# Low parts of moving operands placed 64, 128 or 192 bytes further on

## The chip, the cores and the metric

One core of a Trainium2 chip runs the whole program. The metric is the device time of one launch in microseconds; the median of three runs of the kernel before is 2188.57 us (2188.35 to 2189.26).

## The reference

Two transformer-like blocks run one after the other on 256 tokens of width 2048, all in float32:

```
first block:  h = rmsnorm(x); proj = h @ w_in          # 16 k-tiles of 128
              y_pool, y_conv, y_attn = three mixers of parts of proj
              mixed = sum_n sigmoid(h @ w_gate[n] + b) * (y_n @ w_branch[n]);  x += rmsnorm(mixed @ w_out)
              h = rmsnorm(x); m = relu(h @ w_up)^2 @ w_down;  x += rmsnorm(m)
second block: h = modulated rmsnorm(x); q, k, v, gates from h @ w_in_2; attention; Fourier mix
              out = rmsnorm(x + gate * ((g_a*y_a + g_b*y_b) @ w_out_2))
```

## The kernel before

Every large product is made in three passes of a reduced float32 format (float32r): each operand is kept as a high part and a low part (what is missing from the high part to the exact value), and high times high, high times low and low times high are added up in PSUM. A weight chunk is 256 rows by 512 columns; it comes by DMA into `raw`, ScalarE writes its high part (line 964) and VectorE its low part (line 1318). The order of the chunks is a fixed list of jobs, and small pieces of other work (transposes, softmax, attention scores) are put between chunks at places that the program works out beforehand.

A job has one of two modes. In mode T the activations are the stationary operand and 512 weight columns move through the array (lines 910 to 912). In mode W the weights are the stationary operand, 128 columns at a time, and the 256 tokens of the activations move ("pass the weights", lines 917 to 919):

```
917  pe.matmul(o, wh, xh[:, ka, :], ...)
918  pe.matmul(o, wh, xl[:, ka, :], ...)
919  pe.matmul(o, wl, xh[:, ka, :], ...)
```

`xh` and `xl` are looked up by the job's operand name in `hi_of` and `lo_of` (lines 404 to 407). Each of the 128 partitions of SBUF has its own addresses, and all that follows is about addresses in bytes within a partition, taken modulo 256. `line(64)` moves the allocation to the next address that is 64 past a multiple of 256. From that, the places are:

- the activations' high and low parts (`op0h`, `op0l`, `op1h`, `op1l`, and `yah`, `hch`, `mgh` with their low parts): 64;
- weights in mode T, high and low: 64;
- weights in mode W: high parts 128, low parts 0;
- `tmp` and the small tensors behind it: 64, the attention tensors `qt`, `ktx` and others: 64.

The low parts are written by VectorE: of x0 on line 1386, of x1 and x2 on line 1404, of the pool and conv operands on lines 1490 and 1713. x0, x1 and x2 are the operands of the first block's projections, of its MLP and of the second block; they use the same buffers one after the other. x1 is used in 16 jobs of mode W, x2 in 12 of mode W and in 6 of mode T, pool and conv in 4 each of mode W with half as many k-tiles.

Of the kernel before, what the change touches and what calls it, by code (L numbers as in the profile page):

```python
# [12 lines left out]
F32 = mybir.dt.float32  # L13
F32R = mybir.dt.float32r
# [119 lines left out]
def program(nc, a, out, scratch_e, scratch_x):  # L134
    ctx = ExitStack()
    with ctx:
# [159 lines left out]
        top = [(nc.sbuf_base + 63) // 64 * 64]  # L296

        def at(name, shape, off, dt=F32):
            return nc.alloc_sbuf_tensor_at(name, shape, dt, offset=off)

        def sb(name, shape, dt=F32):
            size = 4 * int(np.prod(shape[1:]))
            t = at(name, shape, top[0], dt)
            top[0] += (size + 31) // 32 * 32
            return t

        raw = [sb(f"raw{i}", [128, KC, 512]) for i in range(NRAW)]
        def line(shift):

            top[0] += (shift - top[0]) % 256  # L310
            return top[0]
# [11 lines left out]
        whi, wlo = split_buffers("whi", 64), split_buffers("wlo", 192)  # L323
        op0_at = line(64)
        op0h, op0l = sb("op0h", [128, 16, 256], F32R), sb("op0l", [128, 16, 256], F32R)
        op1_at = line(64)
        op1h, op1l = sb("op1h", [128, 16, 256], F32R), sb("op1l", [128, 16, 256], F32R)
        tmp_at = top[0]
        tmp = [sb(f"tmp{i}", [128, 512]) for i in range(6)]
        ident = sb("ident", [128, 128])  # L330
# [15 lines left out]
        def bg(name, shape, kb, dt=F32):  # L346
            return at(name, shape, big + int(kb * 1024), dt)
# [18 lines left out]
        x0 = bg("x0", [128, 2, 2048], 52)  # L366
# [12 lines left out]
        hch, hcl = bg("hch", [128, 16, 256], 40, F32R), bg("hcl", [128, 16, 256], 56, F32R)  # L379
# [23 lines left out]
        fgb = at("fgb", [128, 2048], op1_at)  # L403
        hi_of = {"x0": op0h, "x1": op0h, "x2": op0h, "pool": op1h, "conv": op1h, "mix": op1h, "hid0": op1h, "hid1": op1h, "hid2": op1h,
                 "hid3": op1h, "att": op1h, "four": op1h, "ya": yah, "ctx": hch, "mg": mgh}
        lo_of = {"x0": op0l, "x1": op0l, "x2": op0l, "pool": op1l, "conv": op1l, "mix": op1l, "hid0": op1l, "hid1": op1l, "hid2": op1l,
                 "hid3": op1l, "att": op1l, "four": op1l, "ya": yal, "ctx": hcl, "mg": mgl}

        columns = {}
# [15 lines left out]
        def half(ps):  # L425
            return ps[:, :].rearrange("p (k t) -> p k t", k=2)
# [3 lines left out]
        def sem(name):  # L430
            return ctx.enter_context(nc.semaphore("s_" + name))
# [20 lines left out]
        s_winr, s_pwm, s_psc, s_phi, s_plo = sem("pool_window"), sem("pool_weight"), sem("pool_scaled"), sem("pool_high"), sem("pool_operand")  # L452
        s_cy, s_chi, s_clo = sem("conv_taps"), sem("conv_high"), sem("conv_operand")
# [853 lines left out]
        def _(v):  # L1307
# [75 lines left out]
            def low_x0(u, j):  # L1383
                k = 2 * u + j
                v.wait_ge(s_x0hi, k + 1)
                i = v.scalar_tensor_tensor(op0l[:, k, :], bank[4 + k % 4][:, 0:256], vat[:, k:k + 1], op0h[:, k, :].bitcast(F32), ALU.mult, ALU.subtract)
                if j:
                    i.then_inc(s_oper, 1)
                elif u == 0:
                    i.then_inc(s_oper0, 1)  # L1390

            def turn_x(u):
                if u < 8:
                    low_x0(u, 0)
                    low_x0(u, 1)
                    return
                s, k = u // 8, 2 * (u % 8)
                h, l, x = (op0h, hch)[s == 1][:, k:k + 2, :], (op0l, hcl)[s == 1][:, k:k + 2, :], half(tmp[2 + u % 2])
                if u == 8:
                    v.wait_ge(s_pe, of["b23"].end)  # L1400
                v.wait_ge(s_turned, u - 7)
                v.tensor_copy(h, x).then_inc(own.sem, own.up())
                v.wait_ge(own.sem, own.n)
                v.tensor_tensor(l, x, h.bitcast(F32), ALU.subtract).then_inc(s_oper, 1)
# [82 lines left out]

            def pool_low(g):
                v.wait_ge(s_phi, g + 1)
                v.tensor_tensor(op1l[:, 2 * g:2 * g + 2, :], half(tmp[5]), op1h[:, 2 * g:2 * g + 2, :].bitcast(F32), ALU.subtract).then_inc(s_plo, 1)  # L1490

            def conv_taps(b, c):
                ct, job = 4 * b + c, of[f"cc{b}"]
# [168 lines left out]
            def fourier_d(g):  # L1662
# [3 lines left out]
                else:  # L1666
# [9 lines left out]
                v.tensor_tensor(op1l[:, 12 + g, :], tmp[5][:, 0:256], op1h[:, 12 + g, :].bitcast(F32), ALU.subtract).then_inc(s_four, 1)  # L1676

            parts = {"vectors_b": vectors_b, "bias_row": bias_row, "index_sum": index_sum, "top_rounds": top_rounds, "pool_window": pool_window, "pool_low": pool_low, "conv_taps": conv_taps,
                     "softmax1_max": softmax1_max, "softmax1_scale": softmax1_scale, "values1": values1, "fold_map": fold_map, "ada_quarters": ada_quarters,
                     "ada_columns": ada_columns, "ctx_var": ctx_var, "ctx_norm": ctx_norm, "ctx_turn": ctx_turn, "row_var": row_var, "row_norm": row_norm, "turn_x": turn_x, "x1_add": x1_add, "mlp_add": mlp_add,  # L1680
                     "turn_qk": turn_qk, "split_kc": split_kc, "rotate": rotate, "softmax2_max": softmax2_max, "softmax2_less": softmax2_less, "softmax2_sum": softmax2_sum,
                     "softmax2_share": softmax2_share, "values2": values2, "values2_low": values2_low, "fourier_d": fourier_d}
# [20 lines left out]
            def ep_cb(job, b0, b1):  # L1703
                blk = job.arg
                if blk:
                    v.wait_ge(s_chi, 2)
                v.wait_ge(s_cy, 4 * blk + 4)
                for i, b in ((0, b0), (1, b1)):
                    v.tensor_tensor(half(tmp[2 + i]), half(b), cu[:, 2 * i:2 * i + 2, :], ALU.mult).then_inc(s_pair[job.pair], 1)
                for i in range(2):  # L1710
                    k = 8 + 4 * blk + 2 * i
                    v.wait_ge(s_chi, 2 * blk + i + 1)
                    v.tensor_tensor(op1l[:, k:k + 2, :], half(tmp[2 + i]), op1h[:, k:k + 2, :].bitcast(F32), ALU.subtract).then_inc(s_clo, 1)

            def ep_br(job, b0, b1):
                n, c = job.arg
# [131 lines left out]
            def ep_o2_last(job, b0, b1):  # L1848
# [14 lines left out]
                def columns(i):  # L1863
# [27 lines left out]
                v.tensor_scalar(X2[:, 1, 768:1536], X2[:, 1, 768:1536], rs, None, ALU.mult).then_inc(s_fin, 1)  # L1891

            eps = {"copy": ep_copy, "vw": ep_vw, "cc": ep_cc, "cb": ep_cb, "br": ep_br, "wo": ep_wo, "up": ep_up, "dn": ep_dn, "qk": ep_qk,
                   "silu": ep_silu, "pb": ep_pb, "pa": ep_pa, "o2": ep_o2}

# [26 lines left out]
            low_x0(0, 1)  # L1922
            low(1)
            turn_x(1)
            low(2)
            turn_x(2)
            x0_norm(0, 1024, 2048)
            x0_norm(1, 1024, 2048)
# [36 lines left out]
```

## Time and profile before

| | |
|---|---|
| median of three runs | 2188.57 us |
| the profiled execution | 2189.04 us |
| its span, first to last instruction | 2187.2 us |
| granted TensorE clock, mean | 0.999 of full speed |
| PE busy | 2177.7 us (100%) |
| VectorE / ScalarE busy | 1548.0 (71%) / 1063.0 us (49%) |
| DMA | 474.97 MB, mean 217 GB/s |

The table is read from the top: the span is some 2 us below the profiled execution's time, and one engine is busy through all of it. Matmuls are pipelined, so that the time of one matmul in the profile is longer than the distance from its start to the start of the next.

### The profile page before, as it was taken

How to read it: one execution, taken by the hardware profiler on the slowest of the kernel's cores; microseconds unless marked ns; L12 is line 12 of the kernel's file. 1: busy time of each engine (PE TensorE's matmuls, PEld its weight loads, DVE VectorE, ACT ScalarE, POOL GpSimd, SP SyncE). 2: the span in 40 equal slices, each digit the busy share in tenths (PEclk: the TensorE clock that was granted, in tenths of full speed). 3: DMA queues.
4: the chain of work that ended last, by engine and by line, in shares of the span. 5: the costliest groups of instructions: out<-in, count | busy, mean ns of one | idle time of the engine just before them, and what ended most of it. 6: DMA issues, size and time to landing. Idle time of an engine off the chain costs nothing.

```text
span 2187.2 us, 37567 instructions
## 1 busy us (share of the span) xinstructions
PE 2177.7 (100%) x15900; PEld 2046.9 (94%) x15900; DVE 1548.0 (71%) x1895; ACT 1063.0 (49%) x1398; POOL 120.0 (5%) x111
## 2 busy tenths in 40 slices
PE   9999999999999999999999999999999999999998
PEld 9999999999999889989988988998889999999987
DVE  7899588888889577544554555555768787777776
ACT  5444445544444566444543443444555555444443
POOL 1000000000000400000000000000101111110001
PEclk9999999999999999999999999999999999999999
DMA  8876676687787956656656656656755545688784
GB/s 275 245 241 200 201 251 220 228 280 258 256 277 265 244 188 184 193 192 194 196 195 193 194 193 196 200 192 203 246 174 164 164 144 170 224 272 282 256 279 155
DMA packets 248480, 474.97 MB, mean 217 GB/s; under 512 B 21974, under 2 KB 26448, under 8 KB 247544
## 3 DMA queue, kind: packets, MB, share of 16 engines
q1 hardware_dynamic: 243032, 454.40, 65.5%
q0 software_dynamic: 5280, 18.17, 2.9%
q8 instruction: 125, 2.05, 0.4%
q14 instruction: 43, 0.35, 0.0%
HBM read 468.30 MB, written 5.78 MB: 217 GB/s over the span
## 4 chain that ended last, share of the span: by engine, by line
PE 97%; DMA 1%; DVE 1%; ACT 0%; issue 0%; SPq 0%; DVEq 0%; POOLq 0%; POOL 0%; ACTq 0%
PE ps L917 21%; PE ps L918 21%; PE ps L919 21%; PE ps L910 10%; PE ps L911 10%; PE ps L912 10%; PE ps L835 1%; DMA raw<-in_w_out 1%; PE ps L758 0%; PE ps L708 0%; DMA raw<-in_w_in 0%; PE ps L745 0%; PE ps L824 0%; PE ps L823 0%; PE ps L825 0%
## 5 line engine op out<-in xcount | busy, mean ns | idle before, releaser
L917 PE MATMUL ps<-op0h,whiW 128*128 128x256 f32 x3376 | 937.3, 278 | 0.1
L919 PE MATMUL ps<-op0h,wloW 128*128 128x256 f32 x3376 | 932.8, 276 | 0.0
L918 PE MATMUL ps<-op0l,whiW 128*128 128x256 f32 x3376 | 932.7, 276 | 0.0
L1318 DVE TENSOR_TENSOR wloW<-raw,whiW 128x1024 fp32r<-128x1024 f32 (+1 forms) x503 | 618.3, 1241 | 313.5 <-ACT whiW L964 311.1
L964 ACT ACTIVATE whiW<-raw 128x1024 fp32r<-128x1024 f32 (+1 forms) x504 | 529.3, 1058 | 586.0 <-PE ps L919 471.2
L917 PEld LDWEIGHTS ps<-op0h,whiW 128*128 128x128 f32 x3376 | 633.8, 188 | 2.5 <-issue 1.3
L918 PEld LDWEIGHTS ps<-op0l,whiW 128*128 128x128 f32 x3376 | 633.9, 188 | 0.6
L919 PEld LDWEIGHTS ps<-op0h,wloW 128*128 128x128 f32 x3376 | 633.8, 188 | 0.0
L1318 DVE TENSOR_TENSOR wloT<-raw,whiT 128x1024 fp32r<-128x1024 f32 (+1 forms) x264 | 319.1, 1217 | 237.7 <-ACT whiT L964 236.5
L964 ACT ACTIVATE whiT<-raw 128x1024 fp32r<-128x1024 f32 (+1 forms) x264 | 274.0, 1046 | 286.2 <-PE ps L912 228.9
L910 PE MATMUL ps<-whiT,op1h 128*128 128x512 f32 x640 | 249.3, 390 | 0.3 <-DVE wloT L1318 0.3
L911 PE MATMUL ps<-wloT,op1h 128*128 128x512 f32 x640 | 249.1, 389 | 0.0
L912 PE MATMUL ps<-whiT,op1l 128*128 128x512 f32 x640 | 249.1, 389 | 0.0
L1345 DVE SCALAR_TENSOR_TENSOR tmp<-raw,csil,tmp 128x512 f32<-128x512 f32 x300 | 209.3, 746 | 1.1
L910 PEld LDWEIGHTS ps<-whiT,op1h 128*128 128x128 f32 x640 | 120.1, 188 | 25.7 <-issue 1.0
L912 PEld LDWEIGHTS ps<-whiT,op1l 128*128 128x128 f32 x640 | 120.1, 188 | 25.0
L911 PEld LDWEIGHTS ps<-wloT,op1h 128*128 128x128 f32 x640 | 120.1, 188 | 24.7
L917 PE MATMUL ps<-op1h,whiW 128*128 128x256 f32 x512 | 141.9, 277 | 0.0
L918 PE MATMUL ps<-op1l,whiW 128*128 128x256 f32 x512 | 141.4, 276 | 0.0
L919 PE MATMUL ps<-op1h,wloW 128*128 128x256 f32 x512 | 141.4, 276 | 0.0
L918 PEld LDWEIGHTS ps<-op1l,whiW 128*128 128x128 f32 x512 | 96.1, 188 | 0.1
L917 PEld LDWEIGHTS ps<-op1h,whiW 128*128 128x128 f32 x512 | 96.1, 188 | 0.1
(314 smaller groups left out, 2106.8 us busy)
## 6 DMA issues: line engine op xcount, KB each, us to landing
raw<-in_w_in SPq DMA_DIRECT2D x256, 512.0 KB, 4.3
raw<-in_w_up SPq DMA_DIRECT2D x128, 512.0 KB, 3.8
raw<-in_w_down SPq DMA_DIRECT2D x128, 512.0 KB, 4.1
raw<-in_w_ada SPq DMA_DIRECT2D x96, 512.0 KB, 4.6
raw<-in_w_gate SPq DMA_DIRECT2D x96, 512.0 KB, 5.1
raw<-in_w_out SPq DMA_DIRECT2D x64, 512.0 KB, 5.3
raw<-in_w_branch SPq DMA_DIRECT2D x48, 512.0 KB, 5.1
raw<-in_w_proj_a SPq DMA_DIRECT2D x24, 512.0 KB, 5.0
```

The costliest lines, as they stand in the source:

```text
L835: mm = pe.matmul(bank[4][:, 256 * e:256 * e + 256], vv[:, st % 2, 128 * kv:128 * kv + 128], keyed[e][:, st, :], start=st == 0, stop=st == 3)
L910: pe.matmul(o, th, h[:, kk, c0:c1], start=first, stop=False, skip_group_check=True)
L911: pe.matmul(o, th, l[:, kk, c0:c1], start=False, stop=False, skip_group_check=True)
L912: mm = pe.matmul(o, tl, h[:, kk, c0:c1], start=False, stop=last, skip_group_check=True)
L917: pe.matmul(o, wh, xh[:, ka, :], start=first and m % 2 == 0, stop=False, skip_group_check=True)
L918: pe.matmul(o, wh, xl[:, ka, :], start=False, stop=False, skip_group_check=True)
L919: mm = pe.matmul(o, wl, xh[:, ka, :], start=False, stop=last, skip_group_check=True)
L964: act.activation(whi[job.mode][q % NSPL][:, :, 0:job.n], raw[i][:, :, 0:job.n], ACT.Copy).then_inc(s_hi, 1)
L1318: v.tensor_tensor(wlo[job.mode][q % NSPL][:, :, 0:job.n], x, h.bitcast(F32), ALU.subtract).then_inc(s_lo, 1)
L1345: op = v.scalar_tensor_tensor(o, w, c, o, ALU.mult, ALU.add)
```

## The change

Three new names lie over the old low buffers, further on by 128, 192 and 64 bytes, and the allocation is moved up by 192 and by 64 bytes so that they have room. The writers on lines 1404, 1490 and 1713 (numbers of before) write to them, and the table `lo_of` gives them to the matmuls. Nothing is added to or taken from any engine's instructions.

```diff
         op0h, op0l = sb("op0h", [128, 16, 256], F32R), sb("op0l", [128, 16, 256], F32R)
+        x1l, x2l = at("x1l", [128, 16, 256], op0_at + 16384 + 128, F32R), at("x2l", [128, 16, 256], op0_at + 16384 + 192, F32R)
+        top[0] += 192
         op1_at = line(64)
         op1h, op1l = sb("op1h", [128, 16, 256], F32R), sb("op1l", [128, 16, 256], F32R)
+        poolcl = at("poolcl", [128, 16, 256], op1_at + 16384 + 64, F32R)
+        top[0] += 64
         tmp_at = top[0]
...
-        lo_of = {"x0": op0l, "x1": op0l, "x2": op0l, "pool": op1l, "conv": op1l, "mix": op1l, ...
+        lo_of = {"x0": op0l, "x1": x1l, "x2": x2l, "pool": poolcl, "conv": poolcl, "mix": op1l, ...
...
-                h, l, x = (op0h, hch)[s == 1][:, k:k + 2, :], (op0l, hcl)[s == 1][:, k:k + 2, :], half(tmp[2 + u % 2])
+                h, l, x = (op0h, hch)[s == 1][:, k:k + 2, :], (op0l, hcl, x1l, x2l)[s][:, k:k + 2, :], half(tmp[2 + u % 2])
...
-                v.tensor_tensor(op1l[:, 2 * g:2 * g + 2, :], half(tmp[5]), ...
+                v.tensor_tensor(poolcl[:, 2 * g:2 * g + 2, :], half(tmp[5]), ...
...
-                    v.tensor_tensor(op1l[:, k:k + 2, :], half(tmp[2 + i]), ...
+                    v.tensor_tensor(poolcl[:, k:k + 2, :], half(tmp[2 + i]), ...
```

After the change the low parts of x1 lie at 192 modulo 256, of x2 at 0, of pool and conv at 128. The first allocation after them, `op1_at`, is again at 64 (256 bytes higher), but `tmp` and the small tensors behind it move from 64 to 128. The large region behind those begins with `line(64)` as before. The mix, MLP-hidden, attention and Fourier operands keep `op1l`.

## Rows read from the trace of the kernel before

**Rows 1.** The page: busy time of the engines, clock in 40 slices.
```profile
PE 2177.7 (100%) x15900; PEld 2046.9 (94%) x15900; DVE 1548.0 (71%) x1895; ACT 1063.0 (49%) x1398; POOL 120.0 (5%) x111
...
PEclk9999999999999999999999999999999999999999
```

**Rows 2.** All that PE waited for, by releaser: total us, times, longest.
```profile
PE ps L931 <- DVE tmp L1910: 1.2, 1, 1.2
PE ps L910 <- DVE wloT L1318: 0.3, 1, 0.3
PE ps L937 <- DMA vst<-in_b_gate: 0.3, 1, 0.3
```

**Rows 3.** Groups of PE instructions by shape: count, busy us, mean ns, idle before.
```profile
L918 PE MATMUL ps<-op0l,whiW 128*128 128x256 f32 x3376 | 932.7, 276 | 0.0
...
L918 PE MATMUL ps<-op1l,whiW 128*128 128x256 f32 x512 | 141.4, 276 | 0.0
...
L912 PE MATMUL ps<-whiT,op0l 128*128 128x512 f32 x192 | 74.9, 390 | 0.0
...
L835 PE MATMUL ps<-keyed,vc 128*128 128x256 f32 x48 | 12.3, 379 | 0.0
...
L912 PE MATMUL ps<-whiT,mgl 128*128 128x256 f32 x32 | 9.0, 282 | 0.0
...
L825 PE MATMUL ps<-qt,op1l 128*128 128x256 f32 x24 | 6.8, 283 | 0.0
```

**Rows 4.** PE by stretch (window, length, busy us, matmuls in it).
```profile
1020.00:1100.00 80.00, 80.00 (x708) 1.00 0.64 197
1965.00:2000.00 35.00, 35.00 (x311) 1.00 0.89 312
...
1110.00:1180.00 70.00, 70.00 (x311) 1.00 0.61 199
...
2174.00:2179.00 5.00, 5.00 (x44) 1.00 0.00 0
```

**Rows 5.** PE in order of time around attention scores (start us, us, instruction).
```profile
1646.26 0.28 PE L917 MATMUL ps<-op0h,whiW 128*128 128x256 f32 x1
...
1646.60 0.28 PE L823 MATMUL ps<-qt,ktx 128*128 128x256 f32 x1
...
1649.36 0.28 PE L825 MATMUL ps<-qt,ktcl 128*128 128x256 f32 x1
1649.47 0.28 PE L917 MATMUL ps<-op0h,whiW 128*128 128x256 f32 x1
...
1649.83 0.28 PE L917 MATMUL ps<-op0h,whiW 128*128 128x256 f32 x1
...
1650.51 0.28 PE L917 MATMUL ps<-op0h,whiW 128*128 128x256 f32 x1
```

**Rows 6.** PE in order of time in a mode-T job of x2.
```profile
1714.80 0.39 PE L910 MATMUL ps<-whiT,op0h 128*128 128x512 f32 x1
...
1716.43 0.39 PE L911 MATMUL ps<-wloT,op0h 128*128 128x512 f32 x1
```

**Rows 7.** The chain that ended last, two merged pieces (start us, us).
```profile
831.33 1.75 PE ps L708 x16
...
1668.72 3.45 PE ps L835 x16
```

**Rows 8.** VectorE: writing low parts, activations' and weights'.
```profile
L1404 DVE TENSOR_TENSOR op0l<-tmp,op0h 128x512 fp32r<-128x512 f32 x16 | 11.1, 693 | 0.5
...
L1318 DVE TENSOR_TENSOR wloW<-raw,whiW 128x1024 fp32r<-128x1024 f32 (+1 forms) x503 | 618.3, 1241 | 313.5 <-ACT whiW L964 311.1
```

More of the change, by code:

```diff
@@ L405, in program @@
                  "hid3": op1h, "att": op1h, "four": op1h, "ya": yah, "ctx": hch, "mg": mgh}
-        lo_of = {"x0": op0l, "x1": op0l, "x2": op0l, "pool": op1l, "conv": op1l, "mix": op1l, "hid0": op1l, "hid1": op1l, "hid2": op1l,
+        lo_of = {"x0": op0l, "x1": x1l, "x2": x2l, "pool": poolcl, "conv": poolcl, "mix": op1l, "hid0": op1l, "hid1": op1l, "hid2": op1l,
                  "hid3": op1l, "att": op1l, "four": op1l, "ya": yal, "ctx": hcl, "mg": mgl}
@@ L1489, in pool_low @@
                 v.wait_ge(s_phi, g + 1)
-                v.tensor_tensor(op1l[:, 2 * g:2 * g + 2, :], half(tmp[5]), op1h[:, 2 * g:2 * g + 2, :].bitcast(F32), ALU.subtract).then_inc(s_plo, 1)
+                v.tensor_tensor(poolcl[:, 2 * g:2 * g + 2, :], half(tmp[5]), op1h[:, 2 * g:2 * g + 2, :].bitcast(F32), ALU.subtract).then_inc(s_plo, 1)
             def conv_taps(b, c):
@@ L1712, in ep_cb @@
                     v.wait_ge(s_chi, 2 * blk + i + 1)
-                    v.tensor_tensor(op1l[:, k:k + 2, :], half(tmp[2 + i]), op1h[:, k:k + 2, :].bitcast(F32), ALU.subtract).then_inc(s_clo, 1)
+                    v.tensor_tensor(poolcl[:, k:k + 2, :], half(tmp[2 + i]), op1h[:, k:k + 2, :].bitcast(F32), ALU.subtract).then_inc(s_clo, 1)
             def ep_br(job, b0, b1):
```

## The prediction

> **What bounds the kernel now.** I read the page's busy times first, then PE's waits, then the groups by shape, then short stretches. PE is busy 2177.7 us of a span of 2187.2, with 15900 matmuls and as many weight loads, at full granted clock in all 40 slices [rows 1]. All that PE ever waited for on another engine or a DMA adds up to under 2 us [rows 2]. So the time is the number of matmuls of each kind times the distance from one start to the next, and an address can matter only through that distance, or by making another engine late enough to stop PE.
>
> The distance is not the "mean ns" of a group: 276 ns for a mode-W matmul and 390 ns for one of mode T [rows 3] hold latency that overlaps with the next one. I get it from stretches with nothing else in them. A stretch of length L that shows n matmuls, each as long as d, has a distance of about (L + d)/n, since those at its edges are counted too. In the MLP's up stage (x1, mode W) that is (80.00 + 0.276)/708 = 0.1134 us; with x2 in mode W 35.276/311 = 0.1134 us; in mode T with 512 columns 70.39/311 = 0.2263 us; in the last mode-T matmuls of 256 columns 5.282/44 = 0.1200 us [rows 3, 4]. The same 256 columns thus cost 113.4 ns in one place and 120.0 ns in another. Attention scores confirm the second figure: from 1646.60 to 1649.36, 23 distances of 256-column matmuls take 2.76 us, 120.0 ns each [rows 5].
>
> What differs between the two? The last mode-T jobs and the scores have stationary and moving operand at the same place modulo 256 (64 and 64). Mode W has the moving operand at 64 and the weights at 128 or 0. So I take "same place" to be worth 120.0 and "64 bytes apart, either way" 113.4: 6.6 ns more where they meet. But it isn't this alone. After the scores, mode W needs a while to come back: 1649.47 to 1649.83 are three distances at 120 ns, and 1649.83 to 1650.51 are six at 113 ns [rows 5]. And one mode-T job of x2 runs at (1716.43 - 1714.80)/7 = 232.9 ns where others at the same places run at 226.3 [rows 4, 6]. There are two levels, 6.6 ns apart, places bear on which one holds, and so does what came before.
>
> **The change part by part.**
>
> *Number of instructions.* No engine gets one more or less, no wait is added, no queue is passed. VectorE's writes of low parts keep shape and type, 693 ns each on line 1404 [rows 8]; the destination is shifted by whole multiples of 64 bytes. I cost this at nothing: there are 24 shifted writes (16 for x1 and x2, 8 for pool and conv), and VectorE has 313.5 us of idle time before its weight splits alone [rows 8], so that even twice their length (24 x 0.69 = 17 us over the whole run) would stay hidden, with PE waiting 0.3 us for that engine today [rows 2]. Without that cover the last low part of each stage would delay the stage's first chunks, some 0.7 us for each of four stages, 3 us.
>
> *x1, line 918.* 16 jobs x 8 chunks x 2 k-tiles x 4 column blocks = 1024 matmuls move a low part, of the 3376 of the group [rows 3]. While one streams, the next weights are loaded. The low part now lies at 192; weights lie at 128 (its own, high) and 0 (the next, low). Both are 64 away, the distance at which mode W has 113.4 ns today. I take no change. Bounds: up, 6.6 ns each, 1024 x 6.6 = 6.8 us for these alone and 20.3 us if all three matmuls of a group fall to the slower level, as the three after the scores do; down, see below.
>
> *x2, line 918.* 12 jobs x 64 = 768 matmuls. The low part lies at 0: 0 from the low weights loaded while it streams, 128 from its own. If what meets is the moving operand and the next weights, this is "same place": 768 x 6.6 = 5.1 us, or 15.2 us if the whole group of three falls. If it is the operand's own weights, it is 128 apart, for which this trace has no row.
>
> *Pool and conv, line 918.* 8 jobs x 8 k-tiles x 4 = 256 of the 512 [rows 3]. The low part lies at 128: same place as its own weights, 128 from the next. The two readings swap: 256 x 6.6 = 1.7 us, or 5.1 us for the group, under the second reading and unknown under the first.
>
> The two readings are not told apart by the rows. The first score matmul after mode W (1646.60) was preceded by a loading of weights at 64 under a moving operand at 64, and the distances up to it are still (1646.60 - 1646.26)/3 = 113 ns [rows 5]; that speaks against the first reading. The three slow ones behind the scores speak against both as a rule for a single pair.
>
> *x2 in mode T.* 6 jobs x 32 = 192 low parts are stationary [rows 3], now at 0 against weights at 64, apart instead of the same. Bounds: 6.6 ns less each, -1.3 us, to all 576 at 232.9, +3.8 us. I take 0, since 226.3 for 512 columns is 113.2 for 256, the lower level already [rows 4].
>
> *tmp moves from 64 to 128.* It feeds transposes and small products of full float32, some 370 matmuls. They run at 1.75/16 = 109.4 ns (line 708) and 3.45/16 = 215.6 ns (line 835) [rows 7] with both operands at 64. Bounds 0 to 370 x 6.6 = 2.4 us; I take 0, as no row shows them at two levels.
>
> *How far down could it go?* The lowest distance per column in the trace is that of line 835: 215.6 ns for 256 columns of full float32. If those are read in two passes, an estimate for one is 107.8 ns, 5.6 less than mode W has. For the 2048 shifted low parts alone that is -11.5 us, for their groups of three -34 us.
>
> On ports, the trace shows two levels for one shape, 113.4 and 120.0 ns [rows 4, 5]. The Trainium skill ("TensorE: Matmul & The Clock Gate", section "Part 2: What happens when you issue a matmul") says that the moving operand and the weight load have independent read ports, and that loading the next weights takes no bandwidth from the running matmul. By that rule addresses can't matter and the time is that of before; the rows show more than it allows, so it does not close the case.
>
> The sum: 0 + 0 + 0 + 0 on the profiled execution's 2189.04 us, which is 0.47 above the median of 2188.57. I state it against the median: 2188.6 us.
>
> **The rivals.**
>
> *A. Same place makes a stage slower.* The mechanism: a low part lies at the same place modulo 256 as the weights loaded beside it, one of the two readers is held back, and the distance goes to 120.0 ns. For it: the only rows at 120.0 are those with same places, and the change makes one such pair in either reading. Against it: history decides too, and one such pair passed at 113. Prices: x2 alone 5.1 us for the low parts or 15.2 for the groups; pool and conv 1.7 or 5.1. It decides once more than 4.4 us is lost, that is from some 660 slow matmuls. Time 2193.7 for the low parts of x2, up to 2203.8 for its groups; with 128 apart slow as well, up to 2208.9.
>
> *B. More distance between high and low helps.* Mode W's 113.4 is itself 5.6 over the estimate above, and the low and high part of the moving operand are now always at the same place. If their succession costs this, shifted low parts run at 107.8: 2188.6 - 11.5 = 2177.1, and less if a whole group gains. Against it: mode T, with another order of the same things, has the same distance per column, 113.2 per 256, which looks like a rate that doesn't hang on place.
>
> *C. The change doesn't act.* The two levels come from how PE got into a stretch, not from places; all steady mode-W stretches stay at 113.4. That is the forecast's number with another reason, and it is counted with it.
>
> **How the numbers follow.** A run of this kernel tells no change from one of over 0.2%, 4.4 us. Forecast with C: 0.38. A: 0.36, nearly all of it over 4.4 us, mostly in 2193 to 2204. B: 0.26, mostly between 2175 and 2184. Range: 2178 to 2206, leaving out the whole-group cases of B (0.07), those of A that take in x1 or several stages (0.08) and some of the far side of B. The likeliest case by itself has 2185 to 2192. Faster 0.26, same 0.38, slower 0.36.
>
> **What would show it.** In the stretch of the up stage, of x2 in mode W and of pool and conv: the distance (L + d)/n. 113.4 in all three confirms the forecast. 115.6 with line 918's mean ns at 283 is A for low parts alone, 120.0 for groups; in x2 it speaks for the next weights, in pool and conv for its own. Under 113 anywhere is B. x0's stretches, which aren't touched, must stay at 113.4. The forecast is wrong if any stage of 768 triples moves by more than 2 ns per matmul, or if PE begins to wait for VectorE.

## The result and the profile after

The changed kernel takes 2230.97 us (median of 4 runs, 2230.70 to 2231.84) against 2188.46 of before (4 runs): 1.0194 times as long, 95% interval 1.0177 to 1.0212, some 42.5 us. The prediction of 2188.6 was wrong, and 2230.97 lies outside its range of 2178 to 2206.

The page of the changed kernel, engines and clock as in [rows 1]:

```profile
PE 2220.2 (100%) x15900; PEld 2088.7 (94%) x15900; DVE 1548.8 (69%) x1895; ACT 1062.9 (48%) x1398; POOL 120.2 (5%) x111
...
PEclk9999999999999999999999999999999999999999
```

What PE waited for, beside [rows 2]:

```profile
PE ps L935 <- DVE tmp L1914: 1.2, 1, 1.2
PE ps L921 <- DVE wloW L1322: 0.3, 1, 0.3
```

The same 15900 matmul records, the same clock, no new wait of any size: 42.5 us more of PE busy time, and no change to speak of on VectorE or ScalarE (1548.8 against 1548.0, 1062.9 against 1063.0 us). The matmuls themselves start further apart. The groups by shape (mode W is on lines 921 to 923 now, mode T on 914 to 916) show which, beside [rows 3]:

```profile
L921 PE MATMUL ps<-op0h,whiW 128*128 128x256 f32 x3376 | 947.2, 281 | 0.3 <-DVE wloW L1322 0.3
L923 PE MATMUL ps<-op0h,wloW 128*128 128x256 f32 x3376 | 946.1, 280 | 0.0
L922 PE MATMUL ps<-op0l,whiW 128*128 128x256 f32 x1584 | 437.5, 276 | 0.0
L922 PE MATMUL ps<-x1l,whiW 128*128 128x256 f32 x1024 | 293.5, 287 | 0.0
...
L922 PE MATMUL ps<-x2l,whiW 128*128 128x256 f32 x768 | 217.8, 284 | 0.0
...
L916 PE MATMUL ps<-whiT,x2l 128*128 128x512 f32 x192 | 75.8, 395 | 0.0
...
L922 PE MATMUL ps<-poolcl,whiW 128*128 128x256 f32 x256 | 71.8, 280 | 0.0
L922 PE MATMUL ps<-op1l,whiW 128*128 128x256 f32 x256 | 70.7, 276 | 0.0
```

Line 922 stays at 276 ns where the low part stayed (x0's 1584, and the 256 of attention and Fourier) and rises to 287, 284 and 280 where it moved. Lines 921 and 923, whose operands did not move, rise on average too, so the neighbours of a low pass are slower as well. Stretches of pure mode W (x0; pool and conv; x1; x2), to be read as in the prediction:

```profile
210.00:320.00 110.00, 110.00 (x973) 1.00 0.72 221
489.00:499.00 10.00, 10.00 (x87) 1.00 0.79 250
1025.00:1115.00 90.00, 90.00 (x747) 1.00 0.60 182
2010.00:2040.00 30.00, 30.00 (x253) 1.00 0.83 280
```

(L + d)/n gives 113.3 ns for x0, 118.1 for pool and conv, 120.9 for x1, 119.7 for x2, where [rows 4] had 113.4. The edges of short windows blur this, so the table takes the start of each matmul from the same trace and adds up the distances by the low part in use:

| low part | groups of three | before, ns each | after, ns each | difference |
|---|---|---|---|---|
| x1, mode W | 1024 | 113.36 | 120.87 | +23.0 us |
| x2, mode W | 768 | 113.47 | 119.61 | +14.2 us |
| pool, conv, mode W | 256 | 113.34 | 117.80 | +3.4 us |
| x2, mode T, 512 columns | 192 | 228.0 | 231.4 | +1.8 us |
| x0, mode W | 1584 | 113.42 | 113.45 | +0.1 us |

That is 42.5 us, as much as the difference of the medians. The two profiled spans differ by 41.9 us (2229.1 against 2187.2), because mode T of the mix and MLP-hidden operands, which did not move, happens to be 0.8 us shorter in the trace after. Nothing is left for another cause. (A few distances of each kind, behind side work, are longer and count in the microseconds, not in the ns.)

The slow stages have a rhythm: the distances are uneven, and the same sequence of them comes again and again. PE in order of time in x1's stage:

```profile
1030.71 0.29 PE L922 MATMUL ps<-x1l,whiW 128*128 128x256 f32 x1
1030.84 0.29 PE L923 MATMUL ps<-op0h,wloW 128*128 128x256 f32 x1
1030.96 0.28 PE L921 MATMUL ps<-op0h,whiW 128*128 128x256 f32 x1
1031.09 0.29 PE L922 MATMUL ps<-x1l,whiW 128*128 128x256 f32 x1
...
1032.40 0.29 PE L921 MATMUL ps<-op0h,whiW 128*128 128x256 f32 x1
1032.53 0.29 PE L922 MATMUL ps<-x1l,whiW 128*128 128x256 f32 x1
```

From 1030.71 to 1032.53 are 15 distances, between 115 and 130 ns; then the same 15 come again. x2's rhythm is 6 long: 120, 121, 123, 116, 118, 122. Pool's is 18 long and nearly repeats after 6: about 117, 121, 118, 116, 117, 117. So the level belongs to a pattern of several matmuls, not to one.

### The profile page after: what moved, and what is told of

Its sections match the earlier page's. It is cut to its first block, busy times and chain, and to the rows that moved or that the text cites. A ratio compares the mean times of both kernels' runs of the same rounds, so it can differ in the third digit from the quotient of the medians.

```text
span 2229.1 us, 37567 instructions
## 1 busy us (share of the span) xinstructions
PE 2220.2 (100%) x15900; PEld 2088.7 (94%) x15900; DVE 1548.8 (69%) x1895; ACT 1062.9 (48%) x1398; POOL 120.2 (5%) x111
## 4 chain that ended last, share of the span: by engine, by line
PE 98%; DMA 1%; DVE 1%; issue 0%; ACT 0%; POOLq 0%; POOL 0%; DVEq 0%; ACTq 0%
PE ps L922 21%; PE ps L923 21%; PE ps L921 21%; PE ps L915 11%; PE ps L916 11%; PE ps L914 11%; PE ps L839 1%; DMA raw<-in_w_in 1%; PE ps L935 0%; PE ps L762 0%; PE ps L712 0%; PE ps L749 0%; PE ps L827 0%; PE ps L828 0%; PE ps L829 0%
## 5 line engine op out<-in xcount | busy, mean ns | idle before, releaser
L921 PE MATMUL ps<-op0h,whiW 128*128 128x256 f32 x3376 | 947.2, 281 | 0.3 <-DVE wloW L1322 0.3
L923 PE MATMUL ps<-op0h,wloW 128*128 128x256 f32 x3376 | 946.1, 280 | 0.0
L922 PE MATMUL ps<-op0l,whiW 128*128 128x256 f32 x1584 | 437.5, 276 | 0.0
L922 PEld LDWEIGHTS ps<-op0l,whiW 128*128 128x128 f32 x1584 | 297.4, 188 | 0.2
L922 PE MATMUL ps<-x1l,whiW 128*128 128x256 f32 x1024 | 293.5, 287 | 0.0
L922 PE MATMUL ps<-x2l,whiW 128*128 128x256 f32 x768 | 217.8, 284 | 0.0
L922 PEld LDWEIGHTS ps<-x1l,whiW 128*128 128x128 f32 x1024 | 193.8, 189 | 0.1
L922 PEld LDWEIGHTS ps<-x2l,whiW 128*128 128x128 f32 x768 | 145.7, 190 | 0.3
L916 PEld LDWEIGHTS ps<-whiT,op1l 128*128 128x128 f32 x640 | 120.1, 188 | 24.9
L914 PEld LDWEIGHTS ps<-whiT,op1h 128*128 128x128 f32 x640 | 120.1, 188 | 24.8
L915 PEld LDWEIGHTS ps<-wloT,op1h 128*128 128x128 f32 x640 | 120.1, 188 | 24.7
```

Of the source, the lines that this page charges most:

```text
L914: pe.matmul(o, th, h[:, kk, c0:c1], start=first, stop=False, skip_group_check=True)
L915: pe.matmul(o, th, l[:, kk, c0:c1], start=False, stop=False, skip_group_check=True)
L916: mm = pe.matmul(o, tl, h[:, kk, c0:c1], start=False, stop=last, skip_group_check=True)
L921: pe.matmul(o, wh, xh[:, ka, :], start=first and m % 2 == 0, stop=False, skip_group_check=True)
L922: pe.matmul(o, wh, xl[:, ka, :], start=False, stop=False, skip_group_check=True)
L923: mm = pe.matmul(o, wl, xh[:, ka, :], start=False, stop=last, skip_group_check=True)
```

## The experiments

Three theories stood at the start. **S**: the step between the places of two moving operands that follow each other costs (before, it was always 0). **W**: the moving operand against the places of the weights, pair by pair, as in the prediction. **N**: other engines' or DMA traffic, to which the change gave another timing.

**A map of places, matmuls alone.** A kernel without any load or other engine beside the matmuls runs mode W's order through all places:

```
CASES = [("W", wh + wl + "B" + xl) for xl in "ABCD" for wl in "ABCD" for wh in "ABCD"]   # A 0, B 64, C 128, D 192
    ...
    pe.matmul(o, wh, xh, ...); pe.matmul(o, wh, xl, ...); pe.matmul(o, wl, xh, ...)       # 24 groups a case
```

> No part of the reference: matmuls alone on buffers filled from x, no DMA and no other engine beside them. First 64 cases of mode W's order (high weights x high operand, high x low, low x high; 24 groups of three, 256 columns), with the high moving part at 64 and the low moving part, the low weights and the high weights at each of 0, 64, 128, 192. Then four cases in another order (all passes with the high moving part of four column blocks, then the four with the low one), then ten of mode T with 512 columns. Theory S (the step between the places of two moving operands that follow each other costs): cases with the low moving part at 64 run at 113.3 ns a matmul wherever the weights are, the others at 117 to 121 wherever the weights are; the other order costs about a quarter of that extra. Theory W (moving operand against weights): what counts is the place of the weights, and the low part at 64 gives 120 as soon as a weight part is at 64; with weights at 128 and 0 a low part at 128 or 0 costs and one at 192 does not. Theory N (neither; DMA or other engines' traffic makes the levels): all cases within 1 ns.

Stretches of it, in this order: before's places (weights at 128 and 0, low part at 64); all four at 64; then before's weights with the low part at 0, at 128 and at 192.

```profile
174.50:181.50 7.00, 7.00 (x64) 1.00 0.00 0
200.00:207.00 7.00, 7.00 (x61) 1.00 0.01 2
38.50:45.50 7.00, 7.00 (x61) 1.00 0.00 0
310.00:317.00 7.00, 7.00 (x62) 1.00 0.00 0
446.50:454.00 7.50, 7.50 (x64) 1.00 0.00 0
```

The DMA share is 0.01 or less, and 64, 61, 61, 62 and 64 (the last in half a us more) matmuls are there. By start times that is 113.4, 119.9, 120.1, 117.9 and 120.9 ns. The changed kernel has 119.6, 117.8 and 120.9 at the same last three places: N is out, since the loss is all there with nothing but matmuls and weight loads running. The loads beside them take longer too, 188 ns each at before's places and 192 with all four at 64; which of the two holds up the other is not shown. The 15-step rhythm of x1 is there too:

```profile
446.94 0.29 PE L87 MATMUL ps<-xl,wh 128*128 128x256 f32 x1
...
448.75 0.29 PE L87 MATMUL ps<-xl,wh 128*128 128x256 f32 x1
```

Of the 64 combinations with the high moving part at 64, exactly two are at 113.3 to 113.4 in this run: weights at 128 and 0 or at 0 and 128, with the low part at 64. Three more lie near 115.6 and all others at 116.7 to 121.1. With no step at all (low part at 64), the weights' places alone span 113.3 to 120.0: S is not enough. With the weights at 128 and 0, x1's low part, 64 bytes away from both, has the worst of its four places (120.9 against 113.4, 117.9 and 120.1 for 64, 128 and 0): W pair by pair is wrong too. For mode T, all at 64 has 226.6 ns and the nine others 228.9 to 233.5.

**Low and high moved together.**

```diff
-        op0_at = line(64)
+        op0_at = line(128)
```

> The kernel before with op0h and op0l both moved from 64 to 128, so that the step from high to low is still a multiple of 256 and the high weights (128) and the moving operand of x0, x1, x2 are at the same place. Theory S: 2188.5 us, mode W of x0, x1, x2 at 113.3 ns. Theory W: 6.6 ns more for two of the three passes or all of them in 3376 groups, 2188.5 + 45 to 67 = 2233 to 2255 us.

2248.53 us, ratio 1.0272 (1.0256 to 1.0287). No step between high and low, and still 60 us lost: S falls as the only cause. The time is inside the 2233 to 2255 of W; what speaks against W is the map, not this run. All of x0, x1 and x2 stand at 119.1 ns. Stretches of x0 and x1:

```profile
200.00:320.00 120.00, 120.00 (x1009) 1.00 0.66 199
1050.00:1130.00 80.00, 80.00 (x674) 1.00 0.61 185
```

The map has the same relative places (weights at 64 and 192, moving parts at 64) at 119.2.

**Distances rotated among the stages.**

```diff
-  x1l ... op0_at + 16384 + 128    x2l ... op0_at + 16384 + 192    poolcl ... op1_at + 16384 + 64
+  x1l ... op0_at + 16384 + 64     x2l ... op0_at + 16384 + 128    poolcl ... op1_at + 16384 + 192
-  top[0] += 64
+  top[0] += 192
```

The last line only gives `poolcl` its room; it puts `tmp` at 0.

> The changed kernel with the distances rotated: x1 64, x2 128, pool and conv 192 bytes. If the cost belongs to the distance and not to the stage, then from the rows after: x1 takes pool's 117.8 ns (1024 groups: 13.6 us more than before), x2 takes x1's 120.9 (768 groups: 17.3 us), pool and conv x2's 119.6 (256 groups: 4.8 us), in all 2188.5 + 36 = 2224 us; the mode-T jobs of x2 add 0 to 2. If it belongs to the stage (weights' traffic, buffers), x1 stays at 120.9, x2 at 119.6, pool and conv at 117.8 and the time at 2231.

2226.78 us, ratio 1.0173 (1.0156 to 1.0190), 3 us over the expected 2224. The values moved with the shift: x1 117.8, x2 120.8, pool and conv 119.8 ns. The stage has no part in it.

```profile
1025.00:1110.00 85.00, 85.00 (x724) 1.00 0.61 189
```

**The passes in another order, at the changed places.**

```diff
-  for m: (wh, xh), (wh, xl), (wl, xh)
+  for m: (wh, xh), (wl, xh)      then      for m: (wh, xl)
```

> The changed kernel with the passes of mode W in another order: for each k-tile first both passes with the high moving part for all column blocks, then the passes with the low one. 2 changes between high and low per 12 matmuls in place of 8. Theory S: the 42 us shrink to about a quarter, 2188.5 + 11 = 2199 us. Theory W: each matmul still has its own weights, the low passes meet high weights (128) alone: x2 (0) is 128 apart, x1 (192) 64 apart, so those two lose nothing and only pool and conv do: about 2190; but the next weights of a high pass are unchanged, so if the pair with the next weights counts the time stays over 2215.

2217.36 us, ratio 1.0129 (1.0114 to 1.0145). Four times fewer changes of moving part took 13.6 of the 42 us back, not three quarters, so S's price per step is wrong. The time is just over the 2215 that was written for a price of the pair with the next weights. The stages don't bear that out: over all twelve matmuls of a k-tile x1 has 117.9 ns, x2 117.3, pool and conv 117.4. x1's low part is 64 bytes from its own and from the next weights, and its stage is the slowest; its high passes, whose places are those of before, have 118.2 ns and its low passes 117.3. The map's cases of this order have 117.9, 116.6 and 117.5 for the same places. So neither a price per step nor a price per pair explains the run.

**A finer map, short weight loads.** Both moving parts at 64, weights at every multiple of 32; mode T with other places; and plain matmuls behind loads of 16 to 128 columns.

> No part of the reference: matmuls alone, as in the first map, now with both moving parts at 64 and the two weight parts at every multiple of 32 (64 cases of mode W), mode T with 512 columns and the stationary parts at every multiple of 32, mode T with both moving weight parts at each of four places, and plain matmuls of 256 and 512 columns behind weight loads of 16 to 128 columns. Theory P (the load of the next weights, read from SBUF beside the moving operand, makes both the levels and the 113.3 itself): with 16 or 32 stationary columns the distance falls to 107 to 110 ns for 256 columns and 213 to 216 for 512, at either place, and rises with the number of columns loaded. Theory R (113.3 and 226.7 are the rate of the moving operand, and only what is over it comes from weights): 113.3 and 226.7 stay with 16 columns. In the fine map, places count in steps of 64 bytes if 32 past a multiple of 64 gives the same as the multiple below; something between or new values otherwise, and a value under 113.3 would be a version that beats the kernel before.

Nothing of it lies under 113.3 ns for 256 columns or 226.6 for 512: those are the lowest of some 190 cases in the two maps. With a weight part at an odd multiple of 32 they have 115.6 to 124.4 ns, and none of them 113.3; 64 bytes is not the grain. Short loads don't free the matmul. Plain matmuls of 256 columns with 16 and with 128 stationary columns, all at 64 (windows as short as these can't tell the two apart, the start times can):

```profile
765.00:768.00 3.00, 3.00 (x28) 1.00 0.02 5
...
793.00:796.00 3.00, 3.00 (x28) 1.00 0.00 0
```

By start times they are at 116.7 and 120.0, with 64 columns at 113.3, and with 512 moving columns the 16-column load is slower (231.7) than the full one (226.7). With the moving operand at 128 it is another order: 113.3 with 16 columns, 116.6 with 64, 117.8 with 128. The distance doesn't rise with the columns loaded and never falls under 113.3, so P as it was written is wrong. R isn't borne out either: 113.3 and 226.7 did not stay in three of its four cases with 16 columns. What is left of R, that 113.3 and 226.7 are a floor, agrees with all cases; that no weight load at all would do better was not tried. Each case ran once and in one order, and the last experiment shows that the case before can matter.

The finer map also has four cases that contradict the first, all with both moving parts at 64: weights both at 0, or both at 128, at 113.4 ns here and at 117.8 there; weights at 0 and 128 at 118.9 here and at 113.3 there; weights at 192 and 0 at 115.6 here and at 120.0 there. Of the places that reached 113.3 in the first map, only before's did it again. That led to the last experiment below.

**Joint places as a forecast.** The changed kernel with low weights moved:

```diff
-        whi, wlo = split_buffers("whi", 64), split_buffers("wlo", 192)
+        whi, wlo = split_buffers("whi", 64), split_buffers("wlo", 128)
```

> The changed kernel with the low weights of mode W at 192 in place of 0. The joint-place theory (the distance is that of the whole pattern of four places, as the map of matmuls alone gives it) says from the first map: x0 and all groups whose low part is at 64, 1968 of them, 118.06 ns (+27.9 us against 113.33), x1 115.67 ns (1024 groups, +7.2, so 16 us less than in the changed kernel), x2 117.77 (+10.2), pool and conv 118.52 (+4.0), mode T of x2 +1.8 as before: 2188.5 + 51.1 = 2239.6 us. If the shift of the low part alone makes x1 slow, x1 stays at 120.9 and the time is about 2255.

2238.45 us, ratio 1.0225 (1.0210 to 1.0240), against 2239.6 expected. x1, whose moving parts lie where the changed kernel has them, went from 120.87 down to 115.6 ns, while x0, which the change had left alone, went from 113.4 up to 118.2; x2 has 117.8, pool and conv 118.5. Stretches of x0 and x1:

```profile
200.00:320.00 120.00, 120.00 (x1017) 1.00 0.67 201
1050.00:1130.00 80.00, 80.00 (x695) 1.00 0.63 194
```

**All at 64.**

```diff
-        whi, wlo = split_buffers("whi", 64), split_buffers("wlo", 192)
+        whi, wlo = split_buffers("whi", 0), split_buffers("wlo", 0)
```

> The kernel before with the weights of mode W at 64, high and low, as in mode T, so that all four places are 64. Joint places: 119.9 ns (map) in all 4016 groups, 12048 x 6.6 = 79.6 us, 2268 us; mode T stays at 226.7. If the level comes from the step between high and low moving parts alone, there is no step and the time is 2188.5.

2266.72 us, ratio 1.0354 (1.0338 to 1.0369): 120.0 ns in every stage of mode W, 226.7 in mode T of the mix and MLP-hidden operands.

```profile
1060.00:1145.00 85.00, 85.00 (x711) 1.00 0.61 185
```

**The room alone, and the other order at before's places.**

```diff
+        top[0] += 192        # behind op0l, every low part where it was
+        top[0] += 64         # behind op1l; tmp at 128
```

> The kernel before with only the allocation of the change: the 192 and 64 bytes of room are left, so that tmp and the small tensors lie at 128, and every low part stays where it was. All theories that put the loss on the matmuls' low parts: 2188.5 us, within 2 us. If the move of tmp costs (identity, transposes, VectorE), the difference shows it, at most 2.4 us by the bounds of the prediction.

2188.87 us, ratio 0.9999 (0.9989 to 1.0009). The move of `tmp` costs nothing that can be measured, and the whole loss comes from the places of the low parts.

> The kernel before (places unchanged) with the passes of mode W in the other order: per k-tile all passes with the high moving part, then all with the low. Joint places: the map has 113.33 ns for this order at these places, so 2188.5 us, within 3 us. It is the base line of the changed kernel in that order (2217.4): the loss there is then 29 us of places alone and not of the order.

2191.31 us, ratio 1.0010 (1.0001 to 1.0020). At good places the other order costs some 2 us, so the loss of the grouped, changed kernel (26 us) is one of places.

**History.**

```
Y = [(128, 0, 64, 64), (0, 128, 64, 64), (0, 0, 64, 64), (128, 128, 64, 64), (128, 0, 64, 0), ...]
X = [(128, 0, 64, 64), (64, 64, 64, 64), (128, 0, 64, 192), (192, 0, 64, 128)]
CASES = [("W", k) for y in Y for x in X for k in (x, y)]      # each y behind each of four x
```

> No part of the reference: matmuls alone in mode W's order. Eight cases (high weights, low weights, high and low moving part at 128,0,64,64; 0,128,64,64; 0,0,64,64; 128,128,64,64; 128,0,64,0; 128,0,64,128; 128,0,64,192; 64,64,64,64), each once behind each of four others. If the distance is a function of the places alone, each case gives one value, whatever ran before. If it is a rhythm that PE falls into, some cases have two values by what ran before; 0,0,64,64 and 128,128,64,64 should (117.8 in one map, 113.4 in the other), while 128,0,64,64 stays at 113.3 and 64,64,64,64 at 120.0 behind all four, as the full kernels need it. The three cases of the changed kernel should be 120.0, 117.8 and 120.9 behind all four.

The same case, weights both at 0 with both moving parts at 64, behind the first and behind the last of `X`:

```profile
163.50:170.50 7.00, 7.00 (x64) 1.00 0.01 2
214.50:221.50 7.00, 7.00 (x62) 1.00 0.00 0
```

The table has the mean distance over whole rhythms, by start times, in the order of `X`.

| weights, moving parts | distance in ns behind each of the four |
|---|---|
| 128, 0 / 64, 64 (before) | 113.3, 113.3, 113.3, 113.3 |
| 0, 128 / 64, 64 | 113.3, 113.3, 113.3, 118.9 |
| 0, 0 / 64, 64 | 113.3, 113.3, 117.8, 117.8 |
| 128, 128 / 64, 64 | 113.3, 117.8, 117.8, 113.3 |
| 128, 0 / 64, 0 (x2 after) | 120.0, 120.0, 120.0, 117.8 |
| 128, 0 / 64, 128 (pool, conv after) | 117.8, 117.8, 117.8, 117.8 |
| 128, 0 / 64, 192 (x1 after) | 120.9, 120.9, 120.9, 120.9 |
| 64, 64 / 64, 64 | 120.0, 120.0, 120.0, 120.0 |

PE falls into one of several rhythms, and for some places which one differs with what ran before. Two values were not expected: 118.9 for weights at 0 and 128, and 117.8 for x2's places after the change, both behind the last of `X`. Each pair ran once here, so that the same predecessor always gives the same rhythm is likely but not shown. Before's places are the only ones here that came back to 113.3 behind all four; the full kernel needs that, since it breaks the stream with side work again and again.

## Why the prediction was wrong

- **The bound, and how to read it: right.** Only the distance between starts could move, it did, and its reading from a stretch held in every kernel. PE's waits stayed under 2 us, and the other engines' busy times as they were.
- **Instructions, VectorE's writes, `tmp`: right.** The room alone is at ratio 0.9999. The shifted writes take as long as before (692 to 693 ns for x1 and x2, 683 to 688 for pool and conv), and PE waits 0.3 us for VectorE's weight splits, as it did.
- **x1: the step that failed.** The sum has four zeros, and the one for x1 was worst. "Both are 64 away, the distance at which mode W has 113.4 ns today. I take no change." It took a level that belongs to the whole pattern of places for the sum of pair rules, learned from two patterns. The pattern 128, 0, 64, 192 has 120.9 ns. That is 23.0 of the 42.5 us, a little over the upper bound of 20.3 given for x1, because the rhythms are not limited to the two levels seen before: single distances reach 130 ns.
- **x2, mode W: rival A's whole-group price.** The sum had 0 here; A had 15.2 us, and 14.2 came. **Pool and conv:** 0 in the sum, 1.7 or 5.1 in A, 3.4 came. Both stages lost, which only A's far end of 2208.9 had. That x2's number came near is in part luck: A meant a steady 120.0, and the stage has a rhythm of 116 to 123 with a mean of 119.6. What is right in A is that places of moving operand and weights against each other count; that one reader is held back where two places meet is not shown, since x1, where none meet, lost most. And they count in rhythms of 6 to 18 matmuls, which slow the neighbours too. The signs were there: three slow matmuls of mode W behind the scores [rows 5], and a mode-T job at 232.9 with others at 226.3 at the same places [rows 4, 6]. All places at 64 also went with the higher level at 256 columns and the lower one at 512. They said that a pair of places does not fix the distance, and the prediction noted it and then went by pairs.
- **x2, mode T:** +1.8 us, inside -1.3 to +3.8, taken as 0.
- **Rival B** had the estimate of 107.8 ns for a floor. Its row was misread: line 835 has 24 matmuls on `vc` (12 heads, two each), and the profile has 48 records of them [rows 3], so that 215.6 ns is half of a full-float32 matmul of 256 columns, and a whole one takes 431 ns. If 107.8 ns is one of its passes, it is one in four. No combination of places in float32r came under 113.3 ns for 256 columns and 226.6 for 512. At the granted 2.4 GHz those are 272 and 544 cycles, 17 for 16 columns; no run explains them.
- **The range** left out the cases in which several stages fall together as a 0.08 remainder. One cause decided all four terms, so their losses came together: the upper bounds that the prediction itself gives for them, 20.3, 15.2, 5.1 and 3.8 us, add up to 44.4, and 42.5 came.
- **The rule of the Trainium skill** that was weighed ("TensorE: Matmul & The Clock Gate", section "Part 2: What happens when you issue a matmul": independent read ports, no bandwidth taken by the next load of weights) does not hold as a forecast for this format. With nothing else running, places alone change the distance between 113.3 and 121.1 ns, and with both moving parts at 64 the places of the weights alone between 113.3 and 120.0 (in steps of 64 bytes). Whether the two reads share a port, or a matmul waits for a slower load of its own weights, no run tells.

What stays open: the rule inside the PE or SBUF that makes a rhythm out of four places. The maps tabulate it, and forecast two full kernels within 1.5 us (2239.6 against 2238.45, 2268 against 2266.72), but no model of banks or ports has been shown. No place tried beats the kernel before.

## What to carry to other kernels

When PE is busy all through and a kernel's time is a count times a distance, addresses are a parameter of that distance, worth here up to 3.5% of the whole (2266.72 against 2188.6). Don't argue it from pairs or from two known cases: time all combinations of places in one small kernel of matmuls alone, in the real order of passes, and each behind different predecessors, and take a combination that is fast behind all of them. And if one cause would act on several stages, its case in the range is their sum.

## What the chip showed unexpectedly

- The same instructions at the same addresses run steadily at 113.3 ns in one place of a program and at 117.8 in another, behind other matmuls (weights both at 0, moving parts at 64).
- A load of 16 stationary columns makes the following matmul stream slower than one of 64: 116.7 against 113.3 ns with all at 64. With the moving operand at 128 it is 113.3 against 116.6.
- Of 64 combinations of places in steps of 64 bytes two reached 113.3 ns in the first map, and only one of them behind every predecessor tried. A shift of 32 bytes counts as well.
- A full-float32 matmul stands in the profile as two records, 215.6 ns apart for 256 columns.
